# Feed-forward of the first block in double chunks, with 7 instead of 8 tile products in three of eight steps of the first matrix and two of eight of the second

## What is computed

```python
D_MODEL, SEQ = 2048, 256
D_FF = 4 * D_MODEL
hn = rmsnorm(h, g_mlp[l])
h = h + jnp.square(jax.nn.relu(hn @ w_ff1[l])) @ w_ff2[l]
```

## Time and profile before

| quantity | value |
|---|---|
| median of 3 runs | 2771.47 us (2771.46 to 2771.71) |
| the profiled execution | 2771.62 us, its span 2769.8 us |
| granted TensorE clock | 0.998 of full |
| PE busy | 2752.5 us (99%), 13086 matmuls |
| DVE busy | 1672.5 us (60%) |
| ACT busy | 1297.7 us (47%) |
| DMA | 508.15 MB, 183 GB/s on average |

### The profile page before, as it was taken

How to read it: one execution, slowest core, us unless ns; L and a number is a source line. 1 busy time by engine, 2 the same in 40 slices (tenths; PEclk the granted TensorE clock), 3 DMA queues, 4 the chain that set the end, 5 groups by cost and what they waited for, 6 DMA issues and landing times.

```text
span 2769.8 us, 30655 instructions
## 1 busy us (share of the span) xinstructions
PE 2752.5 (99%) x13086; PEld 2289.0 (83%) x13086; DVE 1672.5 (60%) x1417; ACT 1297.7 (47%) x1400; POOL 14.8 (1%) x28
## 2 busy tenths in 40 slices
PE   9999999999999999999999999999999999999999
PEld 7888778888888888888888888888788888888887
DVE  5445765455455545454555675665788488658765
ACT  5335663345554344343344544344655355435553
POOL 0000000000000000000000000000000000000000
PEclk9999999999999999999999999999999999999999
DMA  7645036555456555655555654555656656656555
GB/s 236 219 147 167 32 108 212 193 187 198 168 175 199 188 190 190 195 185 189 191 183 189 218 193 141 183 165 169 214 197 213 197 183 198 209 179 204 182 181 173
DMA packets 257847, 508.15 MB, mean 183 GB/s; under 512 B 9571, under 2 KB 20401, under 8 KB 256817
## 3 DMA queue, kind: packets, MB, share of 16 engines
q1 hardware_dynamic: 255520, 495.62, 54.4%
q0 software_dynamic: 2016, 10.36, 1.2%
q10 hardware_dynamic: 176, 0.23, 0.0%
HBM read 504.08 MB, written 2.10 MB: 183 GB/s over the span
## 4 chain that ended last, share of the span: by engine, by line
PE 86%; ACT 1%; DVE 1%; DMA 0%; issue 0%; SPq 0%; ACTq 0%
PE acc L775 21%; PE acc L776 21%; PE acc L780 21%; PE acc L1389 3%; PE acc L1394 3%; PE acc L1390 3%; PE tb L1389 3%; PE tb L1394 3%; PE tb L1390 3%; PE tb L761 2%; PE acc L1041 0%; PE tb L1092 0%; ACT prob L1783 0%; PE tb L1375 0%; PE acc L983 0%; PE acc L980 0%
## 5 line engine op out<-in xcount | busy, mean ns | idle before, releaser
L2117 DVE TENSOR_TENSOR wlo<-raw,whi 128x2048 fp32r<-128x2048 f32 (+1 forms) x405 | 920.1, 2274 | 670.7 <-ACT whi L1545 670.0
L1545 ACT ACTIVATE whi<-raw 128x2048 fp32r<-128x2048 f32 (+1 forms) x405 | 769.7, 1902 | 707.6 <-PE acc L780 524.3
L775 PE MATMUL acc<-whi,ahi 128*128 128x512 f32 (+1 forms) x1968 | 767.4, 391 | 0.4 <-DVE alo L2226 0.4
L776 PE MATMUL acc<-whi,alo 128*128 128x512 f32 (+1 forms) x1968 | 762.0, 388 | 0.0
L780 PE MATMUL acc<-wlo,ahi 128*128 128x512 f32 (+1 forms) x1968 | 484.2, 387 | 0.0
L775 PEld LDWEIGHTS acc<-whi,ahi 128*128 128x128 f32 x1968 | 370.6, 188 | 75.3 <-DVE wlo L2223 0.9
L776 PEld LDWEIGHTS acc<-whi,alo 128*128 128x128 f32 x1968 | 370.5, 188 | 73.9
L780 PEld LDWEIGHTS acc<-wlo,ahi 128*128 128x128 f32 x1968 | 367.2, 188 | 75.4
L775 PE MATMUL acc<-whi,bhi 128*128 128x512 f32 x824 | 322.2, 391 | 0.0
L776 PE MATMUL acc<-whi,blo 128*128 128x512 f32 x824 | 320.7, 389 | 0.0
L780 PE MATMUL acc<-wlo,bhi 128*128 128x512 f32 x824 | 203.9, 389 | 0.0
(11 more groups left out here) (386 smaller groups left out, 2538.1 us busy)
## 6 DMA issues: line engine op xcount, KB each, us to landing
raw<-in_w_ff SPq DMA_DIRECT2D x128, 1024.0 KB, 5.1
raw<-in_w_in SPq DMA_DIRECT2D x119, 1024.0 KB, 5.1
raw<-in_w_down SPq DMA_DIRECT2D x28, 1024.0 KB, 5.1
raw<-in_w_up SPq DMA_DIRECT2D x44, 512.0 KB, 3.9
raw<-in_w_gate SPq DMA_DIRECT2D x44, 512.0 KB, 4.9
rawx<-in_w_up SPq DMA_DIRECT2D x44, 512.0 KB, 3.8
rawx<-in_w_gate SPq DMA_DIRECT2D x44, 512.0 KB, 4.7
raw<-in_w_out SPq DMA_DIRECT2D x16, 1024.0 KB, 5.2
```

The source lines that it names most:

```text
L775: nc.tensor.matmul(out_(t), hi[:, kt, tt(t)], whi[:, slot, wc(k)], start=first and k == 0, stop=False)
L776: nc.tensor.matmul(out_(t), lo[:, kt, tt(t)], whi[:, slot, wc(k)], start=False, stop=False)
L1545: nc.scalar.activation(whi[:, g % SPLIT, 0:n_], raw_of(n)[:, at:at + n_], ACT.Copy).then_inc(w_hi, 1)
L2117: V.tensor_tensor(wlo[:, g % SPLIT, 0:n_], raw_of(load_of(g))[:, at:at + n_], whi[:, g % SPLIT, 0:n_].bitcast(F32), ALU.subtract).then_inc ...
```

## The change

The feed-forward of the first block runs in double chunks too. A block is now two double chunks of `w_ff1` with plan `DDSDSDSD` (11 items) and two of `w_ff2` with plan `DDSDDSDD` (10 items). The hidden activations are the left operand of `w_ff2`, so their tiles must be built with sums for every block: 8 pairs of tiles, by four half turns (4 transposes each) in the second double chunk of `w_ff1` and four in the first of `w_ff2`. The `raw` ring of the feed-forward has three slots. Relu and the square are both on ACT now. The last chunk outputs go to `h` by `add_ff` after the folds. The first two chunks of the second block's `w_in_2` are interleaved (`SIDE`). The double chunk of the second block is rewritten for the same functions (another order of quarters, Silu on the other side), with the same count of matmuls.

```diff
+FF1_PLAN, FF2_PLAN, GUD_PLAN = "DDSDSDSD", "DDSDDSDD", "DDSDSDSD"
+        for _ in range(2):
+            double(FF1_PLAN, (0, 1, 2))
+        for _ in range(2):
+            double(FF2_PLAN, (0, 1, 2))
...
+        TURN_STEP = (2, 3, 4, 5)
+        BUILD = ({2: "in", 3: "sum", 4: "rest"}, {4: "in", 5: "sum rest"}, {5: "in", 6: "sum", 7: "rest"},
+                 {7: "in sum", 8: "rest"})
...
 PE
             for n in range(3):
-                chunk(bhi, blo, 4, hook=None)
-                turn_chunk(h, n, C_XO + n)
+                chunk(ohi, olo, 4, hook=None)
+                turn_tiles(n, C_XO + n)
...
             def ff(i, first=False, last=False):
-                for n in range(1, 4):
-                    chunk(ahi, alo, hook=lambda n=n: turn_hid(n - 1))
-                chunk(bhi, blo, hook=lambda: turn_hid(3), need=(0, 3))
+                double_chunk(ff1_t, *((tail, {0: 2, 2: 2, 4: 2, 6: 1, 7: 0}) if first else ()))
+                double_chunk(ff1_t, {step: lambda n=n: turn_ff(n) for n, step in enumerate(TURN_STEP)}, {})
+                double_chunk(ff2_t, {step: lambda n=n: turn_ff(n) for n, step in enumerate(TURN_STEP)},
+                             {0: 0, 4: 2, 5: 2, 6: 1, 7: 0})
+                double_chunk(ff2_t, {step: lambda n=n: turn_fin(n) for n, step in enumerate(FIN_STEP)} if last else {}, {})
...
 ACT
+            def tiles_in(t, pairs, src, g=None):
+                act.wait_ge(turn_ready, w.val("turn", 1))
+                        last = nc.scalar.activation(into, of, ACT.Copy)
+            def tiles_hi(t, pairs):
+                act.wait_ge(f_sum, w.n["built"])
+                nc.scalar.activation(t.hi[:, t.part(pairs), :], t.f[:, t.part(pairs), :], ACT.Copy
+                                     ).then_inc(turn_hi, 1)
+            def relu_squares():
+                act.wait_ge(acc_free[c % 2], c // 2 + 1)
+                for n, e in enumerate(ff_e):
+                    for t in range(TT):
+                        if n or t:
+                            act.wait_ge(q_free, 2 * d + 1 + n)
+                        last = nc.scalar.activation(e[:, t, :], e[:, t, :], ACT.Relu, scale=rstd[:, R_MLP, t:t + 1])
+                    last.then_inc(relu_done, 1)
+                    act.wait_ge(relu_done, 2 * w.n["ff"] + n + 1)
+                    nc.scalar.activation(e[:, :, :], e[:, :, :], ACT.Square).then_inc(ff_hid, 1)
...
 DVE
+            def tiles_sum(t, pairs):
+                dve.wait_ge(f_in, w.n["built"])
+                    if t.plan[p] == "S":
+                        link(V.tensor_tensor(f(4), f(3), f(2), ALU.subtract))
+                        linked()
+                        link(V.tensor_tensor(f(5), f(4), f(1), ALU.subtract))
+                        last = V.tensor_tensor(f(3), f(1), f(3), ALU.subtract)
+                        linked()
+                        last = V.scalar_tensor_tensor(f(6), f(5), -1.0, f(0), ALU.mult, ALU.subtract)
+                    else:
+                        last = V.tensor_tensor(f(4, 2), f(2, 2), f(0, 2), ALU.subtract)
+            def tiles_lo(t, pairs):
+                dve.wait_ge(turn_hi, w.val("turn", 1))
+                V.tensor_tensor(t.lo[:, part, :], t.f[:, part, :], t.hi[:, part, :].bitcast(F32), ALU.subtract
+                                ).then_inc(turned, 1)
...
             for n in range(3):
                 block_of(1, ev=add_h(n + 1), early=True)
-                gturn(ahi, alo, "g_mlp", n)
+                two_pairs = (2 * n, 2 * n + 1)
+                tiles_sum(ff1_t, two_pairs)
+                tiles_lo(ff1_t, two_pairs)
```

More of the change, by code:

```diff
@@ L141, in __init__ @@
     def __init__(self):
-        self.n = dict(group=0, chunk=0, turn=0, link=0, used=0, hid=0, gate=0, double=0, built=0)
+        self.n = dict(group=0, chunk=0, turn=0, link=0, used=0, double=0, built=0, plain=0, ff=0, gud=0)
     def val(self, name, off=0, div=1, mul=1):
@@ L205, in item_kinds, with tile_at, step_item @@
-def item_kinds():
[L207 to L215, removed]
+def tile_at(plan):
+    return [sum(NTILE[k] for k in plan[:n]) for n in range(len(plan) + 1)]
+def step_item(plan):
+    return [n + plan[:n].count("S") for n in range(len(plan) + 1)]
@@ L226, in load_slots, with at, part @@
 def load_slots():
[L228 to L234, removed]
-        before.append(m)
[L236 to L241, removed]
+    slot, before, landed, held, turn = [], [], [], {}, 0
+    for n, g in enumerate(ITEM_OF):
+        turn = 0 if n == 0 or RING[g] != RING[ITEM_OF[n - 1]] else turn + 1
+        at = RING[g][turn % len(RING[g])]
+        m = held.get(at)
+        slot.append(at)
+        before.append(m)
+        landed.append((landed[m] if m is not None else 0) + 16 * LOADS[g])
+        held[at] = n
+    return slot, before, landed
+SLOT, BEFORE, LANDED = load_slots()
+@dataclass
+class Tiles:
+    plan: str
+    hi: object
+    lo: object
+    f: object
+    def at(self, pair):
+        return tile_at(self.plan)[pair]
+    def part(self, pairs):
+        return slice(self.at(pairs[0]), self.at(pairs[-1] + 1))
 DHEAD = {"nsa": DK, "mla": NOPE + ROPE}
@@ L763, in turn @@
                 w.n["turn"] += 1
+                w.n["plain"] = w.n["turn"]
             def pieces(src, c0, n=GKT):
@@ L1379, in hid2 @@
-            def hid2(c0, n=GKT):
-                return [e2[:, 1 - t, c0 + k * P:c0 + (k + 1) * P] for k in range(n) for t in range(TT)]
-            def turn_hid2(half):
-                half_turn(hid2(half * 2 * P, 2), (hid2_ready, w.val("double")))
-            def with_hi(o, tile, slot, quad, start=False):
-                nc.tensor.matmul(o, fhi[:, tile, :], whi[:, slot, col(quad)], start=start, stop=False)
-                nc.tensor.matmul(o, flo[:, tile, :], whi[:, slot, col(quad)], start=False, stop=False)
@@ L1898, in _ @@
-                h_turn(n, R_MLP, "g_mlp", C_XO, ahi)
-            def ff(i, first=False, last=False):
-                for n in range(4):
-                    hook = (lambda: turn(bhi, 4 * (n - 1))) if n else None
-                    if n == 0 and first:
-                        hook = lambda: (h_turn(3, R_MLP, "g_mlp", C_XO, ahi), root(R_MLP))
-                    block_of(4, hook,
-                             lambda: take(lambda t: hid1[n % 2][:, t, :], ACT.Relu, R_MLP))
-                block_of(4, lambda: turn(bhi, 12))
-                for n in range(1, 4):
-                    block_of(4, (lambda: fin_turn(n - 1)) if last else None)
```

661 lines of the change are left out of this document (381 added, 280 removed).

## The result

| quantity | before | changed |
|---|---|---|
| median | 2771.59 us (2771.46 to 2771.85, 4 runs) | 2787.95 us (2785.52 to 2788.38, 4 runs) |
| ratio | | 1.0057, 95% interval 1.0043 to 1.0071 |
| profiled execution's span | 2769.8 us | 2786.2 us |

A forecast was written before the change was run, and what follows sets the result against it. PE's issue was taken to bound the kernel, with DVE nearly full in double chunks. Terms -27.2 + 3.0 + 28.4 + 12.9, less 0.5, gave +16.6 us: 2788 us predicted, range 2769 to 2798.

The forecast's parts named there:

- Removed, and moved turns: On PE: 120 matmuls fewer, -27.2 us; transposes in half turns instead of turns, +3.0 us.
- DVE's sum: DVE's work in the second double chunk: 41.2 of the 43.6 us PE has, fitting in sum but not in order.
- The waits of a steady block: PE waits in the two tile-building double chunks of a feed-forward block: 7.1 us a block, 28.4 in four.
- ledger: The instruction-by-instruction replay in time of PE, ACT and DVE through the double chunks, from which the waits were forecast.
- The path: PE waits for item 7, last T item and last item's lo in second double chunk, for `ff_lo` in third.
- the start of the feed-forward: First double chunk: a 4.4 us wait for DVE's add, then 8.5 us in seven places: +12.9 us.
- Second block: 0, at most 1 us either way: Second transformer block: same functions and counts, folds and tail pair reordered; no change, at most 1 us either way.
- The lead holds: Feed-forward: PE waits as little as in earlier double chunks, all waits below 18.7 us; 2749 us, chance 0.12.
- Half the waits: Feed-forward: waits of 3.5 us a block and 8 at the start; 2769 to 2774 us, chance 0.11.
- Loads bind: Tile-building double chunks: loads land later than 5.1 us, each paying 2 us more; 2804 us, chance 0.07.
- wait 1.7: End of the second double chunk: PE waits 1.7 us for DVE's lo of item 10.

The follow-up runs named there:

- repeated profile: The changed kernel run and profiled once more with no edit: 2787.21 us.
- ring experiment: Against the changed kernel, the feed-forward's raw ring goes through its slots as 2, 1, 0 instead of 0, 1, 2: 2784.01 us.

## Why the prediction was right

**Where the time went.** From 2769.8 to 2786.2 us of span is +16.4, where +16.6 was predicted. By stretch: +1.6 before the feed-forward, +11.9 in it (714.3 to 726.2), +2.9 behind it. The repeated profile has -1.2, +12.8 and +2.5, in all +14.2. The prediction had all its 16.6 us in the feed-forward, but for a turn of 0.9 us that the change moves out of it into `w_in_2` (eight transposes of `h`): 15.7 inside it. So it has 3 to 4 us too much there, 2 us too little behind it, and nothing for the start, where two executions differ by 2.8 us. The kind and the place of the loss were foreseen; that the total agrees to 0.2 us is luck.

**The steps one by one.** *Removed, and moved turns:* a double chunk without tiles takes 41.48 and 42.16 us, and 41.5 and 42 were predicted. *DVE's sum:* 41.2 us were predicted for the second double chunk, 40.2 measured. *The waits of a steady block:* 48.9 and 45.9 us were predicted for the two double chunks with tiles, 48.6 and 45.7 came; 178.5 for the block, 178.0 came. The ledger also told what five experiments would give: 175.4, 174.2, 173.5, 172.7 and 172.1 us a block against 175.67, 174.49, 173.23, 172.53 and 171.90. *The path:* the kernel that rounds B first removed just the wait for item 7 and the one of the third double chunk, and left the others.

**The term that was mis-sized** is the start of the feed-forward: 12.9 us of waits on top of the 42.5 of a double chunk with two half turns is 55.4 us for the first double chunk, and 53.2 and 54.7 came; the first block was put at 193 us, and 190.3 and 191.1 came. The 4.4 us wait for the add was there (3.7 in the row, 4.1 from matmul to matmul where 0.23 is normal), half of it by the slot, as the ring experiment shows. Behind it 8.5 us in seven places were predicted; 6.9 came (8.1 in the repeated profile), with what the matmuls at half clock cost. The view has three waits there, 1.25, 2.11 (3.0 predicted) and 0.66 us. At the T item of step 4 the matmul starts 0.5 us behind the one before, where 0.23 is normal, so the wait there was 0.3 us. PE ran seven matmuls at half clock after the long wait; that ACT and DVE caught up meanwhile is likely, but was not tested. With 0.5 us less than predicted in a steady block too, all waits of the feed-forward cost 37.0 us (37.9 in the repeated profile), where 28.4 + 12.9 - 0.5 = 40.8 were predicted.

**The term that failed** is "Second block: 0, at most 1 us either way". That stretch takes 2.9 and 2.5 us more. Windows of it before and after, from the first matmul of `w_in_2` to that of the first gated double chunk, and that double chunk to the first half turn of the next:

```profile
1521.21:1950.50 429.29, 429.29 (x2017) 358.57 (x2016) 269.56 (x235) 203.52 (x235) 1.61 (x3) 1.00 0.56 185
1950.50:2018.19 67.69, 64.66 (x285) 52.23 (x284) 57.54 (x54) 38.53 (x42) 0.00 (x0) 1.00 0.56 186
```

```profile
1534.74:1965.68 430.94, 430.51 (x2025) 359.23 (x2024) 278.55 (x244) 205.00 (x231) 1.62 (x3) 1.00 0.57 188
1965.68:2034.96 69.28, 66.06 (x286) 53.45 (x285) 56.07 (x53) 38.17 (x37) 0.00 (x0) 0.98 0.52 168
```

The first is 1.65 us longer. 0.9 us of it are the eight transposes that stood in the feed-forward before and belong to the moved turns; the rest is probably PE's wait for ACT's `z` (0.4 us in the view), which was not there before and for which no experiment was made. The second is 1.6 us longer, and 0.9 in the repeated profile, where its clock is 1.00. The tail of the norm there runs on the same hooks as in the feed-forward, where the ledger had the root behind DVE's lo; I carried nothing of that over. With the variance one hook earlier it is shorter than before the change:

```profile
1963.19:2030.28 67.09, 64.70 (x285) 52.23 (x284) 56.07 (x53) 38.09 (x37) 0.00 (x0) 1.00 0.54 173
```

So the missing terms are 0.9 to 1.6 us in this double chunk, where the place of the variance gives back 1.5 to 2.2, and some 0.8 us in `w_in_2`. What comes behind is 0.35 us shorter than before. This error and the mis-sized start pull the total in opposite ways, and that is why they hardly show in it.

**The rivals.** *The lead holds* is out: PE waited 26.4 us by the view of waits, over the 18.7 at which it decides, and 37.0 by the time they cost. *Half the waits* put them at 22 us, 3.5 in a steady block; some 6.5 came there, and some 4.2 in the kernel with B first. *Loads bind* is out: in the second block loads land in 4.7 to 6.4 us, 4.9 in the median. Between the first matmul of the feed-forward and its end ACT waits once for one of its loads (3.3 us at 1349.84), and PE doesn't wait behind it. With ACT's rounding of B moved 5.5 us earlier, the load came last in two blocks, and even there the rounding started 0.4 us after the start of the double chunk.

## What to carry to other kernels

Where a helper engine's work is some 90% of the stretch of the engine that sets the time, its sum alone doesn't tell: replay its list in order against the others with durations from the rows, and look for round trips, an instruction queued behind one that waits for the other engine. Try to move those before you take work away. Here taking it away (two S steps) gave 19 us; the same instructions at other places gave 20 us, and with three more such moves and another table the change went from 16 us of loss to 15 us of gain. When a helper (a hook table, a tail) is shared between two stages, cost it in each. And compare a forecast with the result stretch by stretch: a total can agree while its terms don't.

## What the runs showed of the hardware

The clock of TensorE fell behind waits, in some executions and not in others at the same place, and what that cost hung on the wait that followed. In the changed kernel's first profile matmuls after the 2.17 us wait at 1078.92 are 0.43 us apart, for some 3 us; the window of eight of them has a granted clock of 0.50, so 1.2 GHz instead of 2.4:

```profile
1079.75:1082.70 2.95, 2.95 (x8) 2.31 (x7) 2.51 (x3) 2.95 (x2) 0.00 (x0) 0.50 0.76 308
```

In the repeated profile the same double chunk ran at full clock, and had a wait for the lo of item 10 in its place:

```profile
1038.32:1086.97 48.65, 44.29 (x200) 35.78 (x199) 40.27 (x39) 30.11 (x29) 0.00 (x0) 1.00 0.48 164
```

The two take 48.61 and 48.65 us. PE's busy time is 1.4 us higher in the first and hides the wait; only the spacing of the matmuls, or the clock of a window, shows which it was. So the prediction's "wait 1.7" for item 10 is right in time, but in the first profile it is found as a wait in only one of the four blocks (1.41 us at 1439.77), and in the repeated one in three.

Where the next wait is shorter the slow matmuls do cost time. In the first double chunk of the first profile there is no slow matmul behind the 2.11 us wait at 852.54, and a wait of 0.66 us for a lo follows. In the repeated profile eight matmuls run 0.43 us apart behind the same wait, no wait follows, and from the last T item's first matmul to the end of the double chunk it takes 9.87 us instead of 9.25. With a longer slow stretch behind the wait for the add as well, the whole double chunk is 54.68 us and not 53.24:

```profile
805.74:860.42 54.68, 47.53 (x194) 37.93 (x193) 45.09 (x48) 34.81 (x40) 0.00 (x0) 0.91 0.48 165
```
